# Who issues the adaLN weight loads during the first projections

## The reference, cut to what matters

```
mod = silu(c) @ w_ada + b_ada            # 6 parts of 2048: shift1, scale1, gate1, shift2, scale2, gate2
h   = rmsnorm(x, norm1_g) * (1 + scale1) + shift1
p   = h @ w_in + b_in                    # [u_fourier 1024 | q | k | v 3x1024 | gate_A 2048 | gate_B 2048]
x   = x + gate1 * (merge(fourier(u), attention(q, k, v)) @ w_out)
x   = x + gate2 * moe(rmsnorm(x) * (1 + scale2) + shift2)      # 16 experts, top 2 of one group
```

## Time and profile before

| what | value |
|---|---|
| median of 3 runs | 1256.79 us (1255.89 to 1257.97) |
| the profiled execution's own time | 1258.28 us |
| its span, first to last instruction | 1256.5 us |
| TensorE busy over the span | 1157.2 us, 92% |
| VectorE, ScalarE busy | 529.3 us (42%), 368.3 us (29%) |
| HBM read over the span | 418.37 MB, 336 GB/s with what is written |
| mean granted clock of TensorE | 0.981 of full speed |

### The profile page before, as it was taken

The page is one execution under the profiler, slowest core; times in us unless marked ns, Lnnn a source line. Parts: engine busy times, 40 slices in busy tenths (PEclk is TensorE's granted clock), DMA queues, the critical chain, the costliest instruction groups (busy, mean ns, idle before and its releaser), DMA issues.

```text
span 1256.5 us, 14314 instructions
## 1 busy us (share of the span) xinstructions
PE 1157.2 (92%) x5593; PEld 689.3 (55%) x5593; DVE 529.3 (42%) x760; ACT 368.3 (29%) x516; POOL 44.2 (4%) x81
## 2 busy tenths in 40 slices
PE   4899999999999999999999999999798889888785
PEld 1565666776766676667887784444243334333232
DVE  0355446555434445455555545124133323413046
ACT  2323324343333333333445544221011111201013
POOL 0000120010000300000000000000000000000000
PEclk9888999999999999999999998999999999999998
DMA  9999999887767998888575468999999999999998
GB/s 362 373 327 344 338 342 332 287 315 279 272 212 255 309 330 318 311 318 301 192 265 170 168 227 329 421 420 421 421 420 421 421 421 421 421 421 421 421 406 320
DMA packets 114147, 423.27 MB, mean 337 GB/s; under 512 B 8864, under 2 KB 9040, under 8 KB 81312
## 3 DMA queue, kind: packets, MB, share of 16 engines
q1 hardware_dynamic: 109456, 410.55, 85.5%
q0 software_dynamic: 4032, 11.22, 2.7%
q10 hardware_dynamic: 592, 0.59, 0.1%
HBM read 418.37 MB, written 3.95 MB: 336 GB/s over the span
## 4 chain that ended last, share of the span: by engine, by line
PE 68%; DMA 27%; DVE 1%; SPq 1%; issue 1%; ACT 1%; POOL 0%; DVEq 0%
PE bank L741 13%; PE bank L743 13%; PE bank L742 12%; PE bank L1119 10%; DMA mraw<-in_w_exp_up 6%; DMA mraw<-in_w_exp_gate 6%; PE bank L720 4%; DMA mraw<-in_w_exp_down 4%; PE bank L1149 3%; DMA raw<-in_w_in 3%; PE bank L1060 2%; DMA raw<-in_w_ada 2%; DMA araw<-in_w_ada 2%; DMA cst<-in_cache_v_ctx 2%; DMA mraw_g<-in_w_exp_down 1%; DMA mraw_g<-in_w_exp_up 1%
## 5 line engine op out<-in xcount | busy, mean ns | idle before, releaser
L1644 DVE TENSOR_TENSOR w_lo<-raw,w_hi 128x1024 fp32r<-128x1024 f32 x192 | 233.5, 1223 | 273.6 <-ACT w_hi L1290 273.2
L1290 ACT ACTIVATE w_hi<-raw 128x1024 fp32r<-128x1024 f32 x192 | 202.0, 1058 | 327.0 <-PE bank L743 227.2
L1119 PE MATMUL bank<-mraw,xg 128*64 128x512 f32 x904 | 233.5, 601 | 18.0 <-DMA mraw<-in_w_exp_up 8.5
L741 PE MATMUL bank<-w_hi,h_hi 128*128 128x512 f32 x512 | 213.9, 418 | 9.7 <-DVE uqkv L1726 6.9
L743 PE MATMUL bank<-w_hi,h_lo 128*128 128x512 f32 x512 | 203.8, 398 | 0.0
L742 PE MATMUL bank<-w_lo,h_hi 128*128 128x512 f32 x512 | 203.5, 397 | 0.0
L1119 PEld LDWEIGHTS bank<-mraw,xg 128*64 128x64 f32 x904 | 73.2, 137 | 137.4 <-issue 133.3
L741 PEld LDWEIGHTS bank<-w_hi,h_hi 128*128 128x128 f32 x512 | 98.3, 192 | 59.7 <-issue 31.7
L1149 PE MATMUL bank<-mraw,hidT 128*64 128x512 f32 x408 | 101.1, 596 | 23.2 <-DMA mraw<-in_w_exp_down 20.9
L743 PEld LDWEIGHTS bank<-w_hi,h_lo 128*128 128x128 f32 x512 | 98.4, 192 | 22.1
L742 PEld LDWEIGHTS bank<-w_lo,h_hi 128*128 128x128 f32 x512 | 98.7, 193 | 19.6 <-issue 1.0
(11 more groups left out here) (263 smaller groups left out, 1161.7 us busy)
## 6 DMA issues: line engine op xcount, KB each, us to landing
raw<-in_w_in SPq DMA_DIRECT2D x64, 1024.0 KB, 5.8
raw<-in_w_ada SPq DMA_DIRECT2D x64, 1024.0 KB, 7.3
mraw<-in_w_exp_up SPq DMA_DIRECT2D x59, 1024.0 KB, 16.0
mraw<-in_w_exp_gate SPq DMA_DIRECT2D x58, 1024.0 KB, 16.0
mraw<-in_w_exp_down SPq DMA_DIRECT2D x51, 1024.0 KB, 16.1
araw<-in_w_ada SPq DMA_DIRECT2D x64, 512.0 KB, 9.1
raw<-in_w_out SPq DMA_DIRECT2D x16, 1024.0 KB, 5.1
raw<-in_w_na_o SPq DMA_DIRECT2D x8, 1024.0 KB, 5.1
```

Of the source, the lines that this page charges most:

```text
L741: nc.tensor.matmul(o, hi[:, k, s], wh, start=k == first, stop=False)
L1119: last = nc.tensor.matmul(out[x * CAP:(x + 1) * CAP], xg[:, q * LOAD_K + kk, e * CAP:(e + 1) * CAP], slab(slot)[:, kk * COL:(kk + 1) * COL ...
L1290: nc.scalar.activation(w_hi[:, u % AHEAD], r, ACT.Copy).then_inc(hi_ready, 1)
L1644: v.tensor_tensor(w_lo[:, u % AHEAD], r, w_hi[:, u % AHEAD].bitcast(F32), ALU.subtract).then_inc(raw_done[n % RAW], 4)
```

## The change

The 8 loads of block 0 stay with SyncE. The 24 adaLN loads 8 to 31 move into ScalarE's list, and SyncE issues projection loads 0 to 12 one behind the other, each waiting only for its own slot. The places in ScalarE's list:

- behind the first parts of block 0 (two high parts, two transposed copies): loads 8 to 11; in blocks 1 and 2, behind the modulation and high(u+1): loads 17 to 19 and 25 to 27
- behind high(u+5): loads 8b + 12 and 8b + 13; behind high(u+6): 8b + 14; behind high(u+7): 8b + 15 and, but for block 2, 8b + 16

Each load keeps its wait for a free slot. Loads, sizes, rings and the lists of the other engines stay as they are.

```diff
+        def ada_block_load(engine, n):
+
+            b, j = n // 8, n % 8
+            if n >= ARAW:
+                engine.wait_ge(ada_done, n - ARAW + 1)
+            for m in (SHIFT1, SCALE1):
+                engine.dma_start(araw[:, n % ARAW, 2 * m:2 * m + 2],
+                                 ada_v[:, 2 * j:2 * j + 2, m * D + b * COL:m * D + (b + 1) * COL]).then_inc(part_landed[n % ARAW], 16)
...
-            for j in range(8):
-                ada_block_load(0, j)
-            dense_load(0)
-            for b in range(1, BLOCKS):
-                for ch, js in ((1, (0, 1, 2)), (2, (3, 4, 5)), (3, (6, 7))):
-                    for j in js:
-                        ada_block_load(b, j)
-                    dense_load(P0_CHUNKS * (b - 1) + ch)
-                dense_load(P0_CHUNKS * b)
+            for n in range(8):
+                ada_block_load(sp, n)
+            for l in range(L_MAIN - 3):
+                dense_load(l)
             for i in range(3):
                 ada_super_load(A_SUPER + i)
                 dense_load(L_MAIN - 3 + i)
...
                     high(1)
                     transposed(6)
                     transposed(7)
+                if b < BLOCKS - 1:
+                    for n in range(1 if b else 0, ARAW):
+                        ada_block_load(act, 8 * b + 8 + n)
                 for n in range(2, 2 * P0_CHUNKS):
                     high(u + n)
+                    if b < BLOCKS - 1 and n >= 5:
+                        for a in ((12, 13), (14,), (15, 16))[n - 5]:
+                            if a < A_SUPER - 8 * b:
+                                ada_block_load(act, 8 * b + a)
```

More of the change, by code:

```diff
@@ L444, in slot_released @@
                     sp.wait_ge(raw_done[n % RAW], 8 * (n // RAW))
[L446 to L453, removed]
             def ada_super_load(a):
```

## The result

| | before | after |
|---|---|---|
| median of 4 runs each | 1257.38 us | 1269.24 us (1268.21 to 1270.3) |
| ratio, 95% interval | | 1.0094 [1.0078, 1.011] |
| profiled execution, its span | 1258.28, 1256.5 us | 1269.50, 1267.7 us |
| end of the stage of the first projections | 158.4 us | 170.2 us |

The time is 11.9 us up, where 15 us up, 1272 us, was forecast. The page of the changed kernel shows the edit itself: ScalarE's queue, q10, now carries 25.76 MB. Of these 0.59 MB were there before, and 25.17 MB are the 24 loads.

What follows compares the result with a forecast made beforehand. TensorE nearly fills the first-projection stage, but SyncE's queue order stalls it each block. Block 0 +8.2, blocks 1 and 2 +2.5 and +4.6, in all +15.3 us, gave 1272 us; range 1252 to 1277.

Steps and rivals of the forecast that it cites:

- The time a block needs without waits, 31.6 us: First-projection stage: a block's adaLN groups, units and modulation transposes at full clock, without waits, sum to 31.6 us.
- The waits in front of units go: Projection loads no longer stand behind adaLN slots, so TensorE's 7.9 us of waits and their clock cost go.
- ScalarE's time costs nothing: ScalarE's 48 added DMA issues, 7 to 9 us a block, fit its idle time: 0, at most 4.3 a block.
- Rival (4): ScalarE held in its issues by a full queue, 4.3 us in each of three blocks: +28, 1285 us; chance 0.07.
- ScalarE issues at T + 1.1, behind the ACTIVATE: Load 12 goes out 1.1 us after T, when the unit before it has been used, its ACTIVATE taking 1.06.
- Landing, shared: 2.35 us of wait: Load 12 shares engines with a projection load, lands at T + 7.3, wanted at T + 4.95; alone the wait is 1.0.
- Clock, 1.7 us for each wait: After each new wait TensorE runs at a lower clock, costing 0 to 2.5 us more; 1.7 taken.
- Block 0's start, +4.8 us: Loads 8 to 11, no longer prefetched, go out at 42.04; groups of 8 and 9 end at 54.7 instead of 49.90.
- Two waits of 2.35 in block 0: TensorE waits for loads 12 and 15, 2.35 us each; 13 is in time, 14 and 16 have 7 us and more.
- Rival (2): Half the cost: waits shared but full clock, or lone with slow clock, 36.3 or 37.0 a block; 1260 us; chance 0.17.
- Rival (1): Waits stay at the lone 1.0 us, clock unaffected, blocks 1 and 2 take 33.6: -8.9, 1248 us; chance 0.18.
- Rival (3): Nothing moves: same bytes, same engines, transfers set the pace, blocks stay as they were; 1257 us; chance 0.08.

Runs made afterwards that it cites:

- e4: Changed kernel's load order, projection loads ahead, but SyncE issues every load and ScalarE none; 1258.42 us, 0.9991 of the kernel before.
- e9: Kernel before, SyncE alone, order changed from adaLN load 16 on: projection loads go in front of adaLN loads that wait for slots; 1249.51 us, 0.9931.
- e10: Changed kernel, but SyncE issues adaLN loads 0 to 15 in the order of before; ScalarE issues only 16 to 31; 1261.18 us, 1.0015 of before.
- e2: Changed kernel with ScalarE's issues from adaLN load 12 on placed one high part earlier; 1263.52 us, 1.004 of the kernel before.
- e3: Changed kernel with adaLN loads 8 to 11 back on SyncE in their old places, ScalarE's later ones one high part earlier; 1261.43 us, 1.002 of before.
- e5: Changed kernel; SyncE holds projection loads 6, 7, 10 and 11 until adaLN loads 12, 13, 15 (20, 21, 23) have landed; 1272.1 us, 1.0127 of before.
- e6: Changed kernel; SyncE holds projection loads 4 and up until adaLN load 15 has landed; 1267.79 us, 1.0076 of the kernel before.
- e8: e3 plus a gate: projection load l, from 4 on, goes out only when adaLN load 2l + 5 has landed; 1264.91 us, 1.0056 of before.

## Why the prediction was right, step by step

**The time a block needs without waits, 31.6 us.** Right: 31.51 in block 2 of e4 and in block 1 of e9.

**The waits in front of units go.** Right: none is left, and the high parts' waits for data went from 73.1 us to none.

**ScalarE's time costs nothing.** Right in effect. The held-up issues of the earlier trace rows came back, now on ScalarE: three lasted 6.60 us, and the next high part stood behind them.

```profile
41.41 6.60 ACTq L442 DMA_DIRECT2D araw<-in_w_ada  x3
48.06 1.06 ACT L1285 ACTIVATE w_hi<-raw 128x1024 fp32r<-128x1024 f32 x1 [6.08 <-issue]
```

TensorE didn't wait for it: in the whole stage it waits for adaLN loads alone. Rival (4) never came near.

**ScalarE issues at T + 1.1, behind the ACTIVATE.** Wrong by the 1.1 us. The issue starts with the ACTIVATE, not behind it:

```profile
103.20 1.06 ACT L1285 ACTIVATE w_hi<-raw 128x1024 fp32r<-128x1024 f32 x1 [3.72 <-PE bank L738]
103.20 1.94 ACTq L442 DMA_DIRECT2D araw<-in_w_ada  x4
```

Loads 8 to 11 went out from 38.90 on, not from 42.04. There the issue was ahead of more than one: the two high parts and the two transposed copies in front of it in the list began at 39.04 and later.

**Landing, shared: 2.35 us of wait.** Mechanism right, size near. Load 20's second half, issued at 103.61, landed 6.3 us later, at 109.9, so T + 6.7 where T + 7.3 was put; the wait was 1.87 us. Two small errors offset each other in it: the first issue was 1.1 us earlier, and the pair took 6.7 us from there instead of 6.2. In the start of block 0 the two queues did share equally, 48 to 52 us of the changed kernel, columns as in the earlier trace rows:

```profile
q1 hardware_dynamic: 393, 0.80, 54.3%
q10 hardware_dynamic: 392, 0.74, 50.8%
```

These are two hardware queues; the earlier trace rows had shown it for a hardware and a software one. The Trainium skill (DMA: Bandwidth & Descriptors, section on queues, rings and completion order) has the engine take turns by packet, and this trace agrees: 393 and 392 packets.

**Clock, 1.7 us for each wait.** This is the term that was sized wrong in blocks 1 and 2. Behind block 0's long waits it held: the unit behind the wait of 4.11 us ran at 0.61 and took 4.6 us instead of 2.9. Behind block 1's waits of 1.87 and 1.49 us the clock never left 1.00.

```profile
56.14:60.70 4.56, 4.56 (x13) 3.36 (x13) 0.00 (x0) 0.00 (x0) 0.00 (x0) 0.61 0.94 344
110.96:113.99 3.03, 3.03 (x16) 2.18 (x12) 0.00 (x0) 0.00 (x0) 0.00 (x0) 1.00 1.05 383
```

The row at 181.77 had shown that this can be: 1.76 us of wait, clock 1.00. The bounds of 0 to 2.5 us were on record; of the three rows the middle one was taken, and the lower bound came. The length of the wait alone would not have given the right choice (see the last section).

**Block 0's start, +4.8 us.** Undersized. Load 9's group ended at 56.1 instead of 54.7. Load 9 landed 0.5 us later than was put, and the clock fell inside the start: the groups of loads 8 and 9 took 1.30 and 1.93 us, where such a group takes 1.06 at full clock.

**Two waits of 2.35 in block 0.** The other term sized wrong. Loads 13, 14 and 15 waited 0.56, 3.40 and 3.92, in all 7.9 us instead of 4.7; load 12 didn't wait, and load 14, which was given 7 us and more, did. In blocks 1 and 2 too there were three waits and not two: loads 21 and 29 came 1.49 and 1.20 us late, and loads 23 and 31 only 0.81 and 0.86. The prediction looked at each load by itself, what goes out beside it, and not at the sum of bytes in front of load 15. Its own floor, 32.5 us of transfers a block, held the hint: a block whose floor is over its work time of 31.6 can't take 4.3 MB more without paying for all of it.

**The sum.** Both as the stretches give it, us without wait, waits, clock and the rest:

| | forecast | measured |
|---|---|---|
| block 0, over 31.6 | 5.2 (start) + 4.7 + 5.1 = 15.0 | 6.6 + 7.9 + 4.5 = 19.0 |
| block 1, over 31.6 | 4.7 + 3.4 = 8.1 | 4.2 + 0.3 = 4.5 |
| block 2, over 31.6 | 4.7 + 3.4 = 8.1 | 3.9 + 0.3 = 4.2 |
| all, less the 15.9 of before | 31.2 - 15.9 = +15.3 | 27.7 - 15.9 = +11.8 |

So the total came out within 3.5 us by two errors of opposite sign, 4.0 us too little in block 0 and 7.5 too much behind it; that it came so near is luck. The mechanism was right in kind (adaLN loads issued late, beside projection loads nobody wants yet). The e10 run shows that the blocks aren't independent, so this split is one of the changed kernel, not a price list.

**Rival (2), waits shared but the clock at full,** describes blocks 1 and 2: it had 36.3 us a block, and they took 36.1 and 35.8. **Rival (1)** had the clock right there but not the waits (33.6 us), and neither fits block 0. **Rival (3), nothing moves,** by which the Trainium skill (DMA page, "Issuing engines are not separate DMA queues") would be all there is to say: that page has the loads interleave on the same 16 engines whoever issues them, and the rows agree. It goes on that a second issuer saves only issue time; here it also took away an order, and cost 0.94%. e9 against before gives the price of order in the other direction, with the same bytes on the same queue: 0.69%.

**What is open.** Of the small waits that stayed in blocks 1 and 2 of e2, only load 20's was followed back to its issue. How much of e10's 78.7 us in blocks 1 and 2 is the head start moved there and how much is late issue isn't shown. Nor is it shown why the wait of 1.0 us before was followed by a stretch at the lower clock while waits of 1.9 us here weren't. Whether ScalarE can issue these loads in any place of its list without a loss isn't shown either: the best of the kernels in which it does, e10 and e3, take 0.15 and 0.20% more than before.

## What to carry to other kernels

Where the bytes of a block take about as long as its matmuls, count the bytes that go out ahead of the last transfer the block needs, over all queues: every load let go early is paid for there, and a second queue lets it go without your saying so. A hand-written order is worth the look at its holes: find the stretch where the DMA rate is near zero and see which wait stands at the queue's head; moving the loads whose slots are already free in front of it brought 9 us without another engine. And holding a queue back by waits on landings was no cure in the three kernels that tried it (e5, e6, e8): at 315 GB/s instead of 371 the engines of e6 had too little under way up to load 15.

## What the runs showed of the hardware

- **ScalarE's list runs ahead into a DMA issue while its ACTIVATE still runs.** Both begin at 103.20 (above), though the ACTIVATE takes 1.06 us. So placing an issue behind an operation delays it by that operation's wait, not by its duration.
- **The length of a wait doesn't tell whether the clock falls.** In the changed kernel it held over waits up to 1.9 us in blocks 1 and 2, and fell in block 0 around waits of 2.0 and 4.1, and of 3.4 and 3.9 us. But in e9 the unit behind a wait of 3.15 us ran at 1.00 and took 2.97 us, and in e4 the group behind a wait of 1.55 us ran at 0.50 and took 1.93 us instead of 1.06. That wait had another of 2.12 us a group before it. The first line is e9's, the second e4's.

```profile
64.51 0.50 PE L743 MATMUL bank<-w_hi,h_hi 128*128 128x512 f32 x1 [3.15 <-DVE uqkv L1728]
...
51.49 1.93 PE L711 MATMUL bank<-araw,cpad 128*32 128x512 f32 x8 [1.55 <-DMA araw<-in_w_ada]
```

- **A dip in the transfer rate.** At 68 to 72 us, with loads pending, the changed kernel moved only 278 GB/s; GpSimd's bias rows were in flight then, on top of the two hardware queues. They alone don't explain it: e2 moved such rows beside the same two queues at 389 GB/s (65 to 72 us). In 60.5 to 62.5, by contrast, nearly nothing was pending (58 GB/s). The cause of the dip wasn't tested.

```profile
68.00:72.00 4.00, 3.44 (x20) 1.85 (x19) 0.97 (x1) 1.06 (x1) 0.00 (x0) 1.00 0.95 278
60.50:62.50 2.00, 2.00 (x14) 0.84 (x13) 0.54 (x1) 1.06 (x1) 0.00 (x0) 1.00 0.34 58
```
